# The 31st expert's rows kept in SBUF and added by TensorE in strips, instead of stored and gathered

## The reference

```
logits = ht @ w_router + b_router                    # 512 tokens, 32 experts
top_val, top_idx = lax.top_k(logits, 4)
gate = softmax(top_val)
for each expert e, over the tokens that chose it:
    hc  = xb @ w1[e] + b1[e]                         # 1024 -> 2048
    glu = minimum(hc[:, :1024], 7);  lin = clip(hc[:, 1024:], -7, 7)
    y   = (glu * sigmoid(1.702 * glu) * (lin + 1)) @ w2[e] + b2[e]     # 1024 -> 1024
out[token] = sum over its four experts of gate * y
x = x + out;  return rmsnorm(x, g_final)
```

## Time and profile before

| | us |
|---|---|
| median of 3 runs | 1796.53 (1795.06 to 1797.18) |
| the profiled execution | 1798.81 |
| its span, first to last instruction | 1796.9 |
| PE busy | 1714.6 (95%) |
| DVE, ACT, POOL busy | 462.2, 385.5, 108.7 |
| DMA | 501.29 MB, mean 279 GB/s |

### The profile page before, as it was taken

How to read it: one execution, slowest core, us unless ns; L and a number is a source line. 1 busy time by engine, 2 the same in 40 slices (tenths; PEclk the granted TensorE clock), 3 DMA queues, 4 the chain that set the end, 5 groups by cost and what they waited for, 6 DMA issues and landing times.

```text
span 1796.9 us, 36282 instructions
## 1 busy us (share of the span) xinstructions
PE 1714.6 (95%) x15650; PEld 953.0 (53%) x15650; DVE 462.2 (26%) x865; ACT 385.5 (21%) x602; POOL 108.7 (6%) x187
## 2 busy tenths in 40 slices
PE   7989999999999999799999999999999999999986
PEld 5766687788788867433434343434333333343332
DVE  4353525424635254570000000000000000010015
ACT  5464232323325334100101010000000000000011
POOL 0010000000000011000000000000000000000013
PEclk9999999999999999899999999999999999999998
DMA  7202221224225313999999999999999999999996
GB/s 240 71 24 82 76 94 62 74 94 164 71 94 187 141 43 98 410 394 397 383 411 398 410 400 410 400 409 405 404 410 399 411 409 403 411 408 401 410 417 233
DMA packets 105759, 501.29 MB, mean 279 GB/s; under 512 B 11644, under 2 KB 22412, under 8 KB 56368
## 3 DMA queue, kind: packets, MB, share of 16 engines
q1 hardware_dynamic: 83904, 461.40, 65.1%
q0 software_dynamic: 8400, 24.57, 4.3%
q10 hardware_dynamic: 13312, 13.12, 2.1%
HBM read 488.41 MB, written 15.20 MB: 280 GB/s over the span
## 4 chain that ended last, share of the span: by engine, by line
PE 67%; SPq 17%; DMA 8%; issue 3%; DVE 3%; ACT 2%; ACTq 0%; POOL 0%; POOLq 0%; DVEq 0%
PE ps L1970 19%; SPq L507 16%; PE ps L1650 9%; PE ps L1651 9%; PE ps L1652 9%; PE ps L1994 9%; DMA ring<-in_w_exp_out 3%; DMA work<-in_w_exp_in 2%; DMA moe<-in_w_exp_out 2%; PE ps L1747 1%; PE ps L1802 1%; PE ps L1821 1%; PE ps L2038 1%; PE ps L1961 1%; PE ps L489 1%
## 5 line engine op out<-in xcount | busy, mean ns | idle before, releaser
L1970 PE MATMUL ps<-ring,moe 128*32 128x512 f32 x3808 | 417.0, 594 | 3.1 <-DMA ring<-in_w_exp_in 3.1
L1970 PEld LDWEIGHTS ps<-ring,moe 128*32 128x32 f32 x3808 | 115.4, 110 | 290.5 <-issue 253.0
L1549 DVE TENSOR_SCALAR moe<-ps 128x768 f32<-128x768 f32 (+1 forms) x32 | 28.0, 875 | 852.0 <-PE ps L1970 852.0
L1994 PE MATMUL ps<-ring,moe 128*32 128x256 f32 x3648 | 202.7, 379 | 1.2 <-DMA ring<-in_w_exp_out 1.2
L1084 DVE TENSOR_TENSOR wl<-raw,wh 128x1024 fp32r<-128x1024 f32 x104 | 126.2, 1224 | 261.1 <-ACT wh L745 261.0
L745 ACT ACTIVATE wh<-raw 128x1024 fp32r<-128x1024 f32 x104 | 109.0, 1057 | 257.5 <-PE ps L1652 256.8
L1994 PEld LDWEIGHTS ps<-ring,moe 128*32 128x32 f32 x3648 | 109.1, 110 | 85.6 <-DMA ring<-in_w_exp_out 2.8
L1650 PE MATMUL ps<-oph,wh 128*128 128x512 f32 x384 | 151.1, 394 | 2.4 <-DVE work L1217 1.6
L1651 PE MATMUL ps<-opl,wh 128*128 128x512 f32 x384 | 150.0, 391 | 0.0
L1652 PE MATMUL ps<-oph,wl 128*128 128x512 f32 x384 | 149.8, 390 | 0.0
L985 ACT ACTIVATE moe<-ps 128x768 f32<-128x768 f32 (+1 forms) x32 | 23.8, 744 | 581.9 <-DVE moe L1549 581.9
(11 more groups left out here) (325 smaller groups left out, 1690.6 us busy)
## 6 DMA issues: line engine op xcount, KB each, us to landing
ring<-in_w_exp_in SPq DMA_DIRECT2D x172, 1024.0 KB, 28.2
ring<-in_w_exp_out SPq DMA_DIRECT2D x86, 1024.0 KB, 28.8
moe<-in_w_exp_in SPq DMA_DIRECT2D x43, 1024.0 KB, 28.7
work<-in_w_exp_in SPq DMA_DIRECT2D x41, 1024.0 KB, 28.7
raw<-in_w_in SPq DMA_DIRECT2D x26, 1024.0 KB, 5.2
work<-in_w_exp_out SPq DMA_DIRECT2D x22, 1024.0 KB, 29.2
moe<-in_w_exp_out SPq DMA_DIRECT2D x20, 1024.0 KB, 28.1
raw<-in_w_ckv SPq DMA_DIRECT2D x8, 1024.0 KB, 5.0
```

The source lines that it names most:

```text
L1549: nc.vector.tensor_scalar(act_n[:, 0:g], ps[:, 0:g, 256:512].rearrange("p j (n a) -> p j a n", a=2), 1.0 - LIMIT, 1.0 + LIMIT, ALU.max, AL ...
L1970: ins = nc.tensor.matmul(ps[32 * s:32 * s + 32, j, :], xt[:, k, 32 * j:32 * j + 32], w[:, s, :, :], start=False, stop=(k == KT - 1), tile_ ...
L1994: ins = nc.tensor.matmul(y_bank(s, j), at[:, a, j, q, :], w[:, a, s, :], start=False, stop=(q == W2 - 1 and a == 1), tile_position=(0, 32 ...
```

## The change

The store to `y_late`, the four gathers, `late_in` and the row numbers `rowl` are gone. In their place:

- `place_rows` makes `pick_30`: for each t, three groups and 32 slots a 0/1 comparison of `rlate` with the slot number, repeated for four strips, times `glate`.
- `gates_turn` makes 16 transposes in place of 4: those of `pick_l` now into bank 2, and 12 of `pick_30` into banks 3, 6 and 7. ACT evicts these twelve in two copies beside `gate_l`'s, into `gate_30` (slot of a group by token, the same in each strip of 32 partitions).
- The 31st expert's y is evicted into `y_30`, from where it isn't sent.
- `rows_30` (TensorE) adds it in PSUM behind `all_own_rows`: in four turns, each of 3 groups times 4 strips. In a turn strip s works on t = (s + turn) % 4 and writes 256 columns of bank 2t + s // 2. Between turns TensorE waits for `strip_done`.
- `late_row` and its wait go from POOL, so rows 12 to 15 are issued directly behind row 11; on TensorE t = 3 ends with row 15; `add_last(0..2)` wait for all 16 increments of `strip_done`, and only `add_last(3)` for `last_done`.

```
-            pool.wait_ge(y_stored, (NE - 1) * 64)
-            for t in range(TT - 1):
-                late_row(t)
...
             for u in range((TT - 1) * TOPK, TT * TOPK):
                 early_row(u)
-            late_row(TT - 1)
...
             def last_step(p):
                 gate_silu(p, CYCLE[2])
                 act.wait_ge(gl_made, 1)
-                nc.scalar.activation(gate_l, ps[:, 6, :], ACT.Copy).then_inc(gl_kept, 1)
-                y_evict(p - 1, CYCLE[1], p * EC + (DOWNS - EC), p - 1)
+                nc.scalar.activation(gate_l, ps[:, 2, :], ACT.Copy).then_inc(gl_kept, 1)
+                nc.scalar.activation(gate_30[:, 0, :], ps[:, 3, :], ACT.Copy).then_inc(gl_kept, 1)
+                nc.scalar.activation(gate_30[:, 1:3, :], ps[:, 6:8, :], ACT.Copy).then_inc(gl_kept, 1)
+                y_evict(p - 1, CYCLE[1], p * EC + (DOWNS - EC), None, y_30)
                 act_keep(p, CYCLE[2])
-                y_send(p - 1, CYCLE[1], y_late, 1, 0)
...
+                slots_30 = iota[:, 0:CAP].rearrange("p (j n) -> p j n", j=GR).unsqueeze(2).to_broadcast([P, GR, 4, 32])
+                for t in range(TT):
+                    chain(nc.vector.tensor_tensor(pick_30[:, t, :, :, :], slots_30, names["rlate"][:, t:t + 1].unsqueeze(2).unsqueeze(3)
+                                                  .to_broadcast([P, GR, 4, 32]), ALU.is_equal))
+                chain.wait()
+                for t in range(TT):
+                    part = pick_30[:, t, :, :, :].rearrange("p j s n -> p (j s n)")
+                    chain(nc.vector.tensor_scalar(part, part, names["glate"][:, t:t + 1], None, ALU.mult))
...
             def add_last(t):
-                dve.wait_ge(last_done, t + 1)
-                if t < TT - 1:
+                if t == TT - 1:
+                    dve.wait_ge(last_done, 1)
+                else:
+                    dve.wait_ge(strip_done, 4 * TT)
                     dve.wait_ge(row_used, TOPK * (t + 1))
...
             def gates_turn():
                 pe.wait_ge(pickl_ready, 1)
                 pe.wait_ge(at_kept, NE - 1)
+                pe.wait_ge(idx_out, NE - 1)
                 for t in range(TT):
-                    ins = nc.tensor.transpose(ps[:, 6, t * P:(t + 1) * P], pick_l[:, t, :, :].rearrange("p h n -> p (h n)"), ident)
+                    nc.tensor.transpose(ps[:, 2, t * P:(t + 1) * P], pick_l[:, t, :, :].rearrange("p h n -> p (h n)"), ident)
+                for j, bank in enumerate((3, 6, 7)):
+                    for t in range(TT):
+                        ins = nc.tensor.transpose(ps[:, bank, t * P:(t + 1) * P], pick_30[:, t, j, :, :].rearrange("p s n -> p (s n)"), ident)
                 ins.then_inc(gl_made, 1)
...
+            def rows_30():
+                for turn in range(4):
+                    if turn:
+                        pe.wait_ge(strip_done, 4 * turn)
+                    for j in range(GR):
+                        for s in range(4):
+                            t = (s + turn) % TT
+                            rows = slice(32 * s, 32 * s + 32)
+                            ins = nc.tensor.matmul(ps[:, 2 * t + s // 2, s % 2 * 256:s % 2 * 256 + 256],
+                                                   gate_30[rows, j, t * P:(t + 1) * P], y_30[rows, j, :], start=False,
+                                                   stop=turn == 3 and j == GR - 1 and t < TT - 1,
+                                                   tile_position=(32 * s, 0), skip_group_check=True)
+                            if j == GR - 1:
+                                ins.then_inc(strip_done, 1)
+
             def last_rows():
-                pe.wait_ge(diag_ready, TT + TOPK)
-                for t in range(TT - 1):
-                    pe.wait_ge(late_in[t], 16)
-                    gated_rows(t, t, late[t], stop=True).then_inc(last_done, 1)
+                rows_30()
+                pe.wait_ge(diag_ready, TOPK)
                 for k in range(TOPK):
                     u = (TT - 1) * TOPK + k
                     pe.wait_ge(row_in[u], 16)
-                    gated_rows(TT - 1, TT + k, y_rows[u])
-                pe.wait_ge(late_in[TT - 1], 16)
-                gated_rows(TT - 1, TT - 1, late[TT - 1], stop=True).then_inc(last_done, 1)
+                    ins = gated_rows(TT - 1, k, y_rows[u], stop=(k == TOPK - 1))
+                ins.then_inc(last_done, 1)
...
-            pe.wait_ge(gl_kept, 1)
+            pe.wait_ge(gl_kept, 3)
             act_turn(NE - 1, CYCLE[2], NE)
             last_down()
             pe.wait_ge(y_kept, NE)
+            pe.wait_ge(y_third, BIG)
             all_own_rows()
```

More of the change, by code:

```diff
@@ L413, in layer_kernel @@
         zero_ready, zero_stored, pool_turn, over_used = (sem(n) for n in ("zero_ready", "zero_stored", "pool_turn", "over_used"))
-        late_in = [sem(f"late_in{n}") for n in range(TT)]
         last_used, diag_ready = sem("last_used"), sem("diag_ready")
         zero_x = sem("zero_x")
-        pickl_ready, gl_made, gl_kept, last_done = (sem(n) for n in ("pickl_ready", "gl_made", "gl_kept", "last_done"))
+        pickl_ready, gl_made, gl_kept, last_done, strip_done = (
+            sem(n) for n in ("pickl_ready", "gl_made", "gl_kept", "last_done", "strip_done"))
         stored = [sem("stored0"), sem("stored1")]
@@ L686, in early_row @@
                                         ).then_inc(row_in[u], 16)
[L688 to L691, removed]
             for u in range(FIRST_ROWS):
@@ L718, in _ @@
                         gather_rows(GR)
-                pool.wait_ge(y_stored, n * 64 + (NE - 1) * 64)
+                pool.wait_ge(y_stored, n * 64 + (NE - 2) * 64)
                 pool.sem_inc(pool_turn, 1)
@@ L997, in y_evict @@
                 if g > 2:
-                    nc.scalar.activation(y_sb[:, 2, :], ps[:, 5, 0:256], ACT.Copy).then_inc(y_third, 1)
-                nc.scalar.activation(y_sb[:, 0:2, :], ps[:, 4, :].rearrange("p (j n) -> p j n", j=2), ACT.Copy).then_inc(y_kept, 1)
+                    nc.scalar.activation(y[:, 2, :], ps[:, 5, 0:256], ACT.Copy).then_inc(y_third, 1)
+                nc.scalar.activation(y[:, 0:2, :], ps[:, 4, :].rearrange("p (j n) -> p j n", j=2), ACT.Copy).then_inc(y_kept, 1)
             def y_send(n, g, dst, tiles, c):
@@ L1492, in place_rows @@
                 chain(nc.vector.tensor_copy(rowi, rowf))
-                chain(nc.vector.tensor_scalar(tmp_l[:, 0:TT], names["rlate"], float(LATE_ROW), 8192.0, ALU.is_lt, ALU.mult))
-                chain.wait()
-                chain(nc.vector.scalar_tensor_tensor(rowl, names["rlate"], float(-LATE_ROW), tmp_l[:, 0:TT], ALU.add, ALU.add))
+                chain(nc.vector.tensor_scalar(names["rlate"], names["rlate"], float(-LATE_ROW), None, ALU.add))
                 chain(nc.vector.tensor_scalar(names["rlast"], names["rlast"], float(-LAST_ROW), None, ALU.add))
@@ L1587, in diagonal @@
                 nc.vector.tensor_scalar(gate_d[n], ident, column, None, ALU.mult).then_inc(diag_ready, 1)
-            for t in range(TT):
-                diagonal(t, names["glate"][:, t:t + 1])
             for k in range(TOPK):
-                diagonal(TT + k, gate[:, TT - 1, k:k + 1])
+                diagonal(k, gate[:, TT - 1, k:k + 1])
             for u in range((TT - 1) * TOPK):
```

15 lines of the change are left out of this document (7 added, 8 removed).

## The result

| | before | after |
|---|---|---|
| median of 8 runs each, us | 1795.97 (1794.02 to 1799.7) | 1800.95 (1800.06 to 1805.4) |
| ratio, 95% interval | | 1.003 (1.0017 to 1.0042) |
| profiled execution, us | 1798.81 | 1800.09 |
| its span, us | 1796.9 | 1798.3 |
| its tail: first gate transpose to the span's end, us | 60.2 | 64.9 |

The change makes the kernel slower, by 0.3%. The forecast, 1790.0 us, was on the wrong side. The two profiled executions differ by 1.4 us of span and the medians by 5.0, because this execution of after came to the tail 3.4 us earlier (the first gate transpose starts at 1733.36; before at 1736.75). Counted from that transpose on, the tail is 4.7 us longer, close to the medians' difference.

A forecast was written before the change was run, and what follows sets the result against it. The expert weight stream was taken to set the pace, leaving only the tail to gain: add of t = 3 from 1789.44 to 1782.95, -6.5, span 1796.9 to 1790.4, median 1790.0 us. Own range 1788.3 to 1792.3, wider range 1787.0 to 1794.5.

The forecast's parts named there:

- They start at 1767.94: On TensorE, the strips of rows_30 follow the last expert's own rows at once, from 1767.94 to 1773.95 us.
- there is no idle stretch any more between 1764 and the end of TensorE's work: Argument against the low clock: apart from row waits, TensorE would not idle from 1764 us on.
- 4.8 us hole: TensorE's standstill from 1767.94 to 1772.76, taken as the cost of store and gather, to leave with them.
- rival 2: Clock drop to 0.50 over own rows and strips: 1795.6 us if throughout, 1792.8 over half the strips; chance 0.09.
- The strips' size: TensorE's 48 small matmuls in rows_30: four abreast, 5.6 us plus three waits of some 0.13, 6.0 us.
- the column strips: Existing TensorE matmuls taken as the strips' model: 24 of 256 columns, four strips side by side, in 2.80 us.
- The DVE's chain: DVE work without a hole from the strips' end: 4.1 plus 4.9, 9.0 us, so add of t = 3 at 1782.95.
- the closing 7.46 us: Work for the last 128 tokens, from the add of t = 3 to the span's end; claimed to stay 7.46 us.
- The rows of t = 3: POOL's gathers of rows 12 to 15 directly follow row 11's; the last lands at 1777.5, and TensorE could end at 1781.05.
- Twelve more transposes, counted at zero: In gates_turn ahead of the last down product: +2.0 us on TensorE, hidden by waits for weights, so zero.
- The cover: TensorE's waits for weights behind the transposes, 0.38 plus 3.7, together 4.1 us, to absorb their 2.0 us.
- TensorE's gain: TensorE's work would end at 1781.05 instead of 1789.42, put at 8.5 us, 1.9 of it not cashed.

The follow-up runs named there:

- e3: The changed kernel without the count's load, the branch and the code for over-full experts on TensorE; 1788.96 us, ratio 0.9954 to the kernel before.
- e4: The kernel before, with the last rows moved into a branch for n == 0 directly behind the count; 1795.76 us, ratio 0.9997 to the kernel before.
- e1_straight: The changed kernel with strips and last rows in a branch for n == 0, ahead of the overflow code; 1789.04 us, ratio 0.9955 to the kernel before.
- e7_rows_held: The changed kernel with the gathers of rows 8 to 15 held until the first turn of strips ended; 1804.85 us, ratio 1.0043 to the kernel before.
- e8_straight_rows_late: e1_straight with the gathers of rows 12 to 15 held until two turns of strips ended; 1793.8 us, ratio 0.9983 to the kernel before.
- e12_before_transposes: The kernel before with its four gate transposes done four times over; 1797.35 us, ratio 1.0007 to the kernel before.
- e5: The changed kernel, unaltered, run again on another chip; 1803.4 us, ratio 1.0035 to the kernel before.
- e6: The changed kernel with 24 more never-executed instructions (12 transposes) in the overflow code that is jumped over; 1796.23 us, ratio 1.001 to the kernel before.
- e2: The changed kernel with the strips moved ahead of the branch, the adding of gathered rows left behind it; 1792.26 us, ratio 0.998 to the kernel before.

## Why the prediction was wrong

The time was forecast 10.95 us too low. 7.9 of it are span (1798.3 for 1790.4), the other 3.05 how the medians lie to the profiled executions: this one reached the tail 3.4 us earlier than before's, which is luck: in the executions above that point lies anywhere from 1731.1 (e3) to 1737.4 us (e4). The tail alone was forecast at 53.7 us (60.2 less 6.5) and took 64.9. The 7.9, by the prediction's steps:

- **The failed step: "They start at 1767.94"**, and with it "there is no idle stretch any more between 1764 and the end of TensorE's work". The own rows ended 3.75 us earlier than taken, but the 9.02 us without instructions put the strips' start 5.27 us late. (Of the 3.75, 3.4 are the early arrival.) The sum took the 4.8 us hole in the earlier trace rows to be the wait for the gathers alone, and so to be gone with it. The wait was what ended last there, but a fetch of instructions stood in the same hole (q8 at 1768.7; none in e4_before_straight, where no code is jumped over ahead of the last rows). With the wait gone and the engines full, it lasted 9.02 us.
- **The clock**, rival 2, follows from the hole: most of two turns at 0.50. The strips took 8.9 us (1773.21 to 1782.11) where the sum had 6.0; of these 2.9 us some 2.0 are the clock (5.40 for the 3.33 of two turns in e1_straight, 1.58 + 0.17 + 1.58).
- **The strips' size.** At full clock a turn takes 1.58 us and all four 6.8, where the column strips gave 6.0. One after another the 12 matmuls of a turn would be 5.55, an estimate (the 22.2 of the prediction by four), so a turn is 3.5-fold, and with the waits between turns 3.3-fold. A wait of TensorE for its own strips is 0.17 us. By the 3.07-fold of the Trainium skill ("TensorE: Matmul & The Clock Gate", "Part 3: Packing small matmuls — row/col tiling") the sum had been 7.6 us with waits; the run stands between the two.
- **The DVE's chain** held: 8.67 us from 1782.25 to 1790.92, and 8.68 in e1_straight, for 9.0. So did "the closing 7.46 us" (7.4 in both).
- **The rows of t = 3**, issued directly behind row 11 at no price: with them and rows 8 to 11 held back, the hole is 4.2 us instead of 9.0 (e7_rows_held). So their early issue had a price, on TensorE's instructions. That it brings no gain wasn't tested: e8_straight_rows_late holds them 1.8 us longer than the store did.
- **Twelve more transposes, counted at zero**: right in the median (e12_before_transposes); they took 1.3 us, not 2.0. The cover is thinner than the earlier trace rows said: in the executions with the slow stretch the last down product has no wait for weights.
- **Two small slips** without effect: TensorE's gain is 8.4 us (1789.42 less 1781.05), not 8.5, and the twelve records of t = 0, 1, 2 in before took 8.06 us, not twice the 5.2 of full clock: only the first of them ran at half pace.

Taken together, -3.75 + 9.02 + 2.9 + 0.14 (the DVE's start behind the strips) - 0.33 = 7.98 us, for the 7.97 by which the add of t = 3 (1790.92) is later than 1782.95.

The mechanism of the gain was right where instructions are in time: e1_straight has 1789.04 and e3_no_branch 1788.96 us for the forecast 1790.0, with a tail 7.2 us shorter than before's in e1 (forecast 6.5). That it fits so well is in part luck: e1's own rows start 1.2 us earlier in the tail than before's, which makes up for the longer strips. On chips C and D the gain isn't there.

The Trainium skill ("Runtime: NRT & Kernel Launch", "Instruction fetch mechanics") has the rule that I passed over: fetching is sequential, in blocks of 16 KiB, and a taken branch to a target outside the current window has to fetch it first. The trace agrees, 4 us and more ahead of one weight load. The same section calls the crossing of a border "mostly hidden". In straight code the trace agrees with that too: e1's packet at 1770.6 has no idle time of TensorE beside it. Right behind the jump it doesn't: the weight loads stood 5.64 and 6.03 us behind the lone one in after and e5, and 3.21 us in e7 with the engines nearly empty.

**Open.** What the "remote" pieces within the strips are (no instruction packet near, gathers being issued). Why the slow stretch in the 31st down product comes: the profiles fit a difference between chips as well as one made by the gathers. And whether e1_straight is faster than before on most chips: it is by 0.45% on one, and 0.07 to 0.08% with an interval that includes none on two. Against the changed kernel its ratio is lower in each comparison, but the two never ran on one chip; what ran beside the changed kernel is e8_straight_rows_late, 9.6 us ahead.

## What to carry to other kernels

When a wait is taken away, ask what else ran in its shadow. The wait's own line names only what came last; look for packets of the instruction queue in the hole, above all behind a branch. Put the code that is executed directly behind a branch, and the rare case out of the way: the jump over it cost 2.2 us (e6) to 9.3 (e5) here, and nothing only where a longer wait stood beside it (before). And a transfer moved earlier isn't free even if nothing waits for it: with the gathers out of the way the same hole was 4.2 us instead of 9.0 (e7).

## What the runs showed of the hardware

- From the start of a q8 packet to TensorE's first instruction behind a hole: 2.5 and 2.4 us (after), 2.5 and 2.5 (e5), 2.6 and 2.8 (e7), 3.0 (e6), 3.1 (e2), 2.3 (e12). The rest of a hole is what passes until the packet starts: with gathers at 398 GB/s, 3.4 us from the lone weight load to the next packet (after); with engines nearly empty, 0.6 us from the same load (e7), and 0.4 us behind the last strip (e2).
- After's page has 126 such packets and 2 times 15,742 TensorE instructions, 250 a packet: an estimate of a border about every 250 instructions, if this queue is TensorE's alone. Where the border falls behind the jump was worth 7.2 us (e6 against e5).
- Four row strips of 32 x 256 in float32 side by side: 12 matmuls in 1.58 us.
